# A one-core decoder trunk: table loads on two queues, VectorE's order in the first row and at a pass border, norm vectors as columns, and the last layer norm in pieces with tanh

## The reference, cut to what matters

```
mod = silu(c) @ w_ada + b_ada                 # 1024 -> 6 x 1024: sh1, sc1, g1, sh2, sc2, g2
h = rms_norm(x, norm1_g) * (1 + sc1) + sh1
qa, ka, va, ub, uc, ud = split(h @ w_in)      # q, k, v | conformer | short conv | pool
ya = diff_attention(qa, ka, va, ...)          # 4 heads, two score maps each, causal
yb = silu(layer_norm(dwconv31(val * sigmoid(gate)) + dw_b, ln_g, ln_b))   # 256 channels
yc = bg * dwconv3(cg * xc)
yd = multiscale_pool(ud) @ pool_w * pool_scale
x = x + g1 * (concat(ya, yb, yc, yd) @ w_out)
h = rms_norm(x, norm2_g) * (1 + sc2) + sh2
x = x + g2 * (square(relu(h @ w_ff1)) @ w_ff2)
```

## Time and profile before

| | before |
|---|---|
| three runs, us | 2376.82 (median), 2379.27, 2375.77 |
| profiled execution, us | 2375.63 |
| its span, us | 2373.8 |
| granted TensorE clock, mean of the span | 0.987 |
| PE busy | 2285.4 us, 96% |
| DVE busy | 1749.2 us, 74% |
| ACT busy | 975.2 us, 41% |
| POOL busy | 354.6 us, 15% |
| chain that ended last, by engine | PE 83%, DVE 8%, DMA 3%, ACT 2% |

### The profile page before, as it was taken

One profiled execution on the slowest core, in us unless ns is written; L12 is line 12 of the kernel. 1 busy time (PEld: TensorE's weight loads), 2 busy tenths in 40 slices (PEclk: granted clock), 3 DMA queues, 4 the chain that ended last, 5 costly groups with the idle time before them and its releaser, 6 DMA issues.

```text
span 2373.8 us, 31336 instructions
## 1 busy us (share of the span) xinstructions
PE 2285.4 (96%) x11618; PEld 1926.3 (81%) x11618; DVE 1749.2 (74%) x2660; ACT 975.2 (41%) x1598; POOL 354.6 (15%) x281
## 2 busy tenths in 40 slices
PE   5999999987999999999999999999999999999999
PEld 3987897766889888888888888888888888888887
DVE  5558796978989876877676767677687676767676
ACT  4532555458888854432322222233432322223231
POOL 0343043823355630000000000000000000000000
PEclk8999999988999999999999999999999999999999
DMA  7441434120000052111111111135101111111112
GB/s 261 156 155 46 151 116 151 49 98 27 15 14 23 10 163 77 54 54 36 62 44 55 51 53 53 53 123 195 63 28 44 62 44 53 53 53 53 53 53 88
DMA packets 108280, 177.68 MB, mean 75 GB/s; under 512 B 5512, under 2 KB 77468, under 8 KB 107164
## 3 DMA queue, kind: packets, MB, share of 16 engines
q1 hardware_dynamic: 108188, 176.45, 22.5%
HBM read 152.84 MB, written 23.59 MB: 74 GB/s over the span
## 4 chain that ended last, share of the span: by engine, by line
PE 83%; DVE 8%; DMA 3%; ACT 2%; issue 2%; POOL 1%; SPq 1%; ACTq 0%; DVEq 0%
PE ps L2486 10%; PE ps L2484 10%; PE ps L2485 10%; PE ps L2522 7%; PE ps L2521 7%; PE ps L2523 7%; PE ps L2187 6%; PE ps L2188 6%; PE ps L2189 6%; PE ps L2374 2%; PE ps L2431 2%; PE ps L2429 2%; PE ps L2430 2%; PE ps L2359 2%; DVE sb_scores L1816 2%
## 5 line engine op out<-in xcount | busy, mean ns | idle before, releaser
L1974 DVE TENSOR_TENSOR sb_x_new<-sb_x_new,ps 128x512 f32<-128x512 f32 x512 | 347.2, 684 | 107.6 <-PE ps L2486 102.0
L2484 PE MATMUL ps<-sb_w_hi,sb_u_hi 128*128 128x512 f32 x1024 | 398.3, 389 | 0.0
L2485 PE MATMUL ps<-sb_w_lo,sb_u_hi 128*128 128x512 f32 x1024 | 398.3, 389 | 0.0
L2486 PE MATMUL ps<-sb_w_hi,sb_u_lo 128*128 128x512 f32 x1024 | 398.3, 389 | 0.0
L2486 PEld LDWEIGHTS ps<-sb_w_hi,sb_u_lo 128*128 128x128 f32 x1024 | 192.3, 188 | 39.9
L2484 PEld LDWEIGHTS ps<-sb_w_hi,sb_u_hi 128*128 128x128 f32 x1024 | 192.3, 188 | 39.9
L2485 PEld LDWEIGHTS ps<-sb_w_lo,sb_u_hi 128*128 128x128 f32 x1024 | 192.3, 188 | 39.8
L2189 PE MATMUL ps<-sb_h_hi,sb_w_lo 128*128 128x512 f32 x512 | 199.4, 389 | 0.0
L1418 ACT ACTIVATE ps<-ps 128x512 f32<-128x512 f32 x28 | 16.3, 582 | 410.8 <-PE ps L2523 410.8
L2187 PE MATMUL ps<-sb_h_hi,sb_w_hi 128*128 128x512 f32 x448 | 178.0, 397 | 0.7 <-DVE sb_w_lo L1935 0.7
L2188 PE MATMUL ps<-sb_h_lo,sb_w_hi 128*128 128x512 f32 x448 | 174.4, 389 | 0.0
(11 more groups left out here) (286 smaller groups left out, 4955.4 us busy)
## 6 DMA issues: line engine op xcount, KB each, us to landing
sb_w_full<-in_w_ff SPq DMA_DIRECT2D x34, 1024.0 KB, 5.1
sb_w_full<-in_w_ff SPq DMA_DIRECT2D x56, 512.0 KB, 3.8
sb_w_raw<-in_w_in SPq DMA_DIRECT2D x16, 1024.0 KB, 5.7
sb_ada<-in_w_ada SPq DMA_DIRECT2D x32, 512.0 KB, 5.3
sb_ada_first<-in_w_ada SPq DMA_DIRECT2D x8, 1024.0 KB, 14.3
sb_x_in<-in_x SPq DMA_DIRECT2D x16, 512.0 KB, 4.9
sb_mix_in<-mix_scratch SPq DMA_DIRECT2D x16, 512.0 KB, 5.1
sb_x_new<-in_x SPq DMA_DIRECT2D x16, 512.0 KB, 4.8
```

The costliest lines, as they stand in the source:

```text
L1974: V.tensor_tensor(out=y, in0=y, in1=psum[:, 4 + p % 4, :], op=ALU.add).then_inc(ff2_read, 1)
L2484: M(dst, uh, wh[:, j, col], start=j == order[0], stop=False, skip_group_check=fast)
L2485: M(dst, uh, wl[:, j, col], start=False, stop=False, skip_group_check=fast)
L2486: ins = M(dst, ul, wh[:, j, col], start=False, stop=j == order[1], skip_group_check=fast)
```

## The change

Six things are moved or replaced; all numbers of the result stay as the reference has them.

- The five tables for the conformer and short convolution, biases and weights, are loaded from ACT's queue, ahead of its first table load, and no longer from SP's. The lambda load goes behind the first `w_ada` slab.
- In the chain of the first row, `w_lo` of the first slab comes behind DVE's gain and no longer ahead of the column extraction; PE transposes the first x tile behind slab 5 and no longer behind slab 7.
- At the end of pass one, the statistics, the row tail and the scaling of the x tiles (`load_squares`, `h_tail`, `scale_rows`) move ahead of three taps and of the short convolution of the next block.
- The shift and gain vectors of the second norm come as eight one-column products of PE, and DVE reads the eight columns directly.
- `load_qk(2)` goes ahead of the store of layer norm (1, 0), and `load_qk(3)` directly behind the load of v.
- Layer norm (1, 1): the reciprocal runs as four pieces of 128 columns, in steps 9 to 12; its two products in steps 13 and 14; ACT's part, one channel half each in steps 16 and 17. In pass two, `Tanh` of half the argument takes the place of `Sigmoid`, and POOL makes 0.5 t + 0.5 of it with a `tensor_scalar` ahead of each product. Its POOL part stands at u = 19 in place of 10, its store behind `load_qk(8)` in place of `load_qk(6)`.

```diff
-                                (R_DWB, R_LNG, conf_dw_b), (R_LNG, R_LNB, conf_ln_g),
-                                (R_LNB, R_PSC, conf_ln_b), (R_PSC, R_END1, pool_scale)):
+                                (R_PSC, R_END1, pool_scale)):
                 sp.dma_start(table1[r0:r1, :], rows(src)).then_inc(tab_ld, 16)
-            for r0, r1, src in ((R_DWW, R_SW, conf_dw_w), (R_SW, R_END2, short_conv_w)):
-                sp.dma_start(table2[r0:r1, :], src.rearrange("o j (a p) -> (o j a) p", p=P)).then_inc(tab_ld, 16)
...
-            sp.dma_start(lam_in[:, :, :], lam_params[0, :, :].partition_broadcast(P)).then_inc(lam_ld, 16)
             for k in range(DC):
                 sp.dma_start(ada_first[k][:, :], w_ada_v[:, k, 0:2 * D]).then_inc(ada0_ld[k], 16)
+                if k == 0:
+                    sp.dma_start(lam_in[:, :, :], lam_params[0, :, :].partition_broadcast(P)).then_inc(lam_ld, 16)
...
+            load_qk(2)
             store_ln(1, 0)
...
             sp.dma_start(v_sb[:, :, :], qkv_v[:, :, 2 * GW:3 * GW]).then_inc(v_ld, 16)
+            load_qk(3)
             sp.dma_start(gate_d[:, :], gate_row[:, 0, :]).then_inc(gate_st, 16)
-            for i in range(2, NT):
+            for i in range(4, NT):
                 load_qk(i)
-                if i == 6:
+                if i == 8:
                     store_ln(1, 1)
...
                     y = acc[:, cc, b * BLK:(b + 1) * BLK]
+                    if h:
+                        half = ln_sig[h][cc][:, :]
+                        link(pool.tensor_scalar(half, half, 0.5, 0.5, ALU.mult, ALU.add))
                     pool.tensor_tensor(out=y, in0=y, in1=ln_sig[h][cc][:, :], op=ALU.mult).then_inc(lnout_ready, 1)
...
-                if u == LN_STEP + 4:
+                if u == LN_STEP + 13:
                     ln_out(1, 1)
...
+            for r0, r1, src in ((R_DWW, R_SW, conf_dw_w), (R_SW, R_END2, short_conv_w)):
+                act.dma_start(table2[r0:r1, :], src.rearrange("o j (a p) -> (o j a) p", p=P)).then_inc(tab_ld, 16)
+            for r0, r1, src in ((R_DWB, R_LNG, conf_dw_b), (R_LNG, R_LNB, conf_ln_g), (R_LNB, R_PSC, conf_ln_b)):
+                act.dma_start(table1[r0:r1, :], src.rearrange("o (a p) -> (o a) p", p=P)).then_inc(tab_ld, 16)
             act.wait_ge(const_ready, 1)
...
-                    A(ln_sig[h][cc][:, :], acc[:, cc, blk], ACT.Sigmoid).then_inc(lnsig_ready, 1)
+                    if h:
+                        A(ln_sig[h][cc][:, :], acc[:, cc, blk], ACT.Tanh, scale=0.5).then_inc(lnsig_ready, 1)
+                    else:
+                        A(ln_sig[h][cc][:, :], acc[:, cc, blk], ACT.Sigmoid).then_inc(lnsig_ready, 1)
...
-                if u == LN_STEP + 4:
-                    ln_silu(1, 1)
+                if u in (LN_STEP + 10, LN_STEP + 11):
+                    ln_silu(1, 1, (u - LN_STEP - 10,))
...
+            def ln_inverse(part):
+                dve.wait_ge(*ln_read(1, 1, 1))
+                rs = ln_rs[1][:, part * P:(part + 1) * P]
+                return mark(V.reciprocal(rs, rs))
+
+            def ln_scale_part(cc, done):
+                y = acc[:, cc, BLK:2 * BLK]
+                dve.wait_ge(dve_chain, done)
+                ins = V.tensor_tensor(out=y, in0=y, in1=ln_rs[1][:, :], op=ALU.mult)
+                if cc == GC - 1:
+                    ins.then_inc(lnz_ready, 1)
...
-                columns(psum[:, 6:8, :], DC, h_tmp[:, :, :].rearrange("p k t -> p (k t)"))
                 r = R_B + (3 + h) * DC
-                vector = V.scalar_tensor_tensor(out=(gain2 if h else shift2)[:, :], in0=diag_sum[:, 0:DC], scalar=float(GW),
+                vector = V.scalar_tensor_tensor(out=(gain2 if h else shift2)[:, :], in0=psum[:, 6, 0:DC], scalar=float(GW),
...
+                    if h == 0 and (cc, b) == (GC - 1, 0):
+                        load_squares(HT + 2)
+                        h_tail(HT, h_tmp)
+                        scale_rows(HT + 2)
                     if h or b == 0:
                         pump(taps, 3)
...
-                    if h == 0 and (cc, b) == (GC - 1, 0):
-                        h_tail(HT, h_tmp)
-                        load_squares(HT + 2)
                     if h == 0 and (cc, b) == (0, 1):
                         h_tail(HT + 1, h_tmp)
-                        scale_rows(HT + 2)
...
-                if u == LN_STEP + 3:
-                    ln_scale(1, 1)
+                if 0 <= u - LN_STEP - 3 < 4:
+                    inverted = ln_inverse(u - LN_STEP - 3)
+                if 0 <= u - LN_STEP - 7 < GC:
+                    ln_scale_part(u - LN_STEP - 7, inverted)
...
+                if k == 5:
+                    transposes(0, x_in[0])
             ins.then_inc(mod1_mm, 1)
-            pe.wait_ge(tab_col, 2)
-            transposes(0, x_in[0])
...
-                for n in range(2):
-                    ins = M(psum[:, 6 + n, :], ones_mean[:, :], mod_sums(h)[1 - s][:, n * BLK:(n + 1) * BLK], start=True, stop=True)
+                if s:
+                    for n in range(2):
+                        ins = M(psum[:, 6 + n, :], ones_mean[:, :], mod_sums(h)[0][:, n * BLK:(n + 1) * BLK], start=True, stop=True)
+                else:
+                    for k in range(DC):
+                        ins = M(psum[:, 6, k:k + 1], mod_sums(h)[1][:, k * P:(k + 1) * P], ones_mean[:, 0:1], start=True, stop=True)
```

More of the change, by code:

```diff
@@ L1554, in _ @@
             add_slice(7)
-            w_in_tail(0)
             dve.wait_ge(mod1_mm, 1)
@@ L1563, in _ @@
                                    op0=ALU.add, op1=ALU.mult).then_inc(mod1_ready, 1)
+            w_in_tail(0)
             V.memset(conf[:, :, 0:TAPS - 1], 0.0)
```

6 lines of the change are left out of this document (3 added, 3 removed).

## The result

The changed kernel took 2357.9 us (median of four runs, 2356.4 to 2361.4); the kernel before it 2378.05 in the same measurement. The ratio is 0.9913 with a 95% interval of 0.9896 to 0.9931. A second measurement of the same code gave 0.9894 (0.9876 to 0.9913). The forecast was 2360.0 with a range of 2352 to 2368. The profiled execution's span fell from 2373.8 to 2354.6 us, by 19.2, and TensorE's mean granted clock rose from 0.987 to 0.993.

What follows compares the result with a forecast made beforehand. TensorE was taken as busy almost throughout, losing time to a few waits in the first 900 us. Terms -7.0 - 1.5 - 2.5 - 2.3 - 3.0 = -16.3 from 2375.63 gave 2359.3, stated as 2360.0 us, range 2352 to 2368.

Steps and rivals of the forecast that it cites:

- Start: Kernel start: earlier DMA stream and reordered first-row chain let PE begin projections at about 40.1 us, -7.0 us.
- Border: Border of the two passes: PE's 5.29 us wait goes, but what follows is late next, -1.5 us.
- Norm vectors: Pass two: two DVE instructions of 1.22 us each go ahead of the gated products PE waits for, -2.5 us.
- rival b: Start gives less: stream doesn't move, or more first projections run at PE's lower clock; 2362 to 2365 us, chance 0.14.
- Attention's start: Head of attention: earlier q/k tile ends ACT's wait, only DVE's idle 2.65 us on the path, -2.3 us.
- Last layer norm: Attention around steps 10 to 12: 9.6 us lost there go, pieces, Tanh and POOL's work cost some back, -3.0 us.
- Rival (c): DVE and POOL's shared port lock: layer norm gives nothing or costs up to 3.5 us; 2363 to 2366.5, chance 0.16.
- (d): Attention gains more, ACT's 6.8 us and most of the 9.6 coming through; 2349 to 2355 us, chance 0.08.
- (e): Start slower: tables issued by ACT queue behind the slabs on the shared DMA engines; up to 2379 us, chance 0.05.

Runs made afterwards that it cites:

- u_tables: Changed kernel with all ten tables back on SP's queue and the lambda load ahead of the first slab again: 2359.95 us, ratio 0.9917.
- u_chain: Changed kernel with `w_lo` ahead of the column extraction and PE's first-row transposes behind slab 7 again: 2363.27 us, ratio 0.9929.
- the repeat: The changed kernel executed and traced once more, no edit: 2356.95 us, ratio 0.9894.
- u_border: Changed kernel with statistics, tail and scaling of the x tiles back behind the taps and the short convolution: 2360.51 us, ratio 0.9924.
- u_norm: Changed kernel with the norm vectors as two products of 512 columns and DVE's column extraction again: 2361.72 us, ratio 0.9930.
- after: The first profiled execution of the changed kernel, no further edit: span 2354.6 us; the kernel's median time 2357.9 us.
- u_qk: Changed kernel with the third and fourth q/k tile loaded behind the layer-norm store, value load and gate store again: 2365.26 us, ratio 0.9926.
- s_sig: Changed kernel with Sigmoid for Tanh in both layer norms of pass two, without POOL's four extra instructions; pieces stay: 2364.63 us, ratio 0.9920.
- before: The profiled execution of the kernel without the change: span 2373.8 us; the kernel took 2378.05 us in the same measurement.

## Why the prediction was right

The sum (-16.3) and the time came out near the measured -19.2 and 2357.9, by the mechanisms named; two of the five terms were clearly too small, a third can't be told apart from what executions differ by, and the errors partly cancel, so that the sum comes as near as this is in part luck. (2359.3 and the 1.2 to the median make 2360.5; the forecast says 2360.0.)

- **Start, -7.0: right.** 7.11 at the first projection, by the rows forecast; u_tables and u_chain share it as 2.3 and 5.4. The 0.9 more in the first rows was not in the sum, and the repeat doesn't have it (0.05).
- **Border, -1.5: right.** 1.0, and 1.65 by u_border. The x tile that I named as late next is the wait; the value weights were not. The mechanism is seen; the -1.5 itself was set between 0 and -5.3 and not worked out.
- **Norm vectors, -2.5: mis-sized.** The term counted DVE's 2.44 us and took PE's clock as given. It measured 4.1, and 4.95 in u_norm. The rest is the lower clock behind the longer wait, which the prediction takes up only as a loss at the start (rival b). In two of ten traces with the changed order the clock fell here all the same.
- **Attention's start, -2.3: not told apart.** 1.0 in after, 1.9 in the repeat; u_qk gives 1.63 for the loads against after and 2.54 against the repeat. DVE's idle 2.65 us did go. POOL's two extra instructions hold PE's first score for 0.9 (I had said 0.4), but s_sig, without them, has none of that left at place 6. What after lacks against the repeat it loses where its four sums of the layer norm run at the lower clock (3.38 against 2.13 us).
- **Last layer norm, -3.0: mis-sized.** 5.2. I counted 9.6 lost and 6.6 given back. By PE's starts 8.7 were won (13.9 at place 6, 22.6 at the product that starts at 549.65 in before) and 3.6 given back by place 7: the term that failed is what the pieces, Tanh and POOL's part cost in the dense steps. POOL's new instruction costs 0.62, not 1.25; how the rest divides no run shows. Before, the granted clock around this hole was 0.68, 0.50 and 0.50 from 540 to 555, after it was 1.00 from 515 to 565; the sum had no term for that.

Rival (c), the lock: its mechanism is seen. The Trainium skill ("SBUF — State Buffer", Who interferes with whom) has DVE and GpSimd block each other on a shared port pair. The trace agrees, and with the full price: in after the ratio instruction takes over 0.3 us ten times between 505 and 745, and each time it ends 0.01 to 0.02 us behind a POOL instruction. It is held until POOL is done, so it pays what is left of POOL's instruction and not always a whole 1.3, and the other 40 of 50 take at most 0.27, so the layer norm still gained. Rivals (d) and (e) didn't come.

Open: what makes the granted clock fall behind one wait of 2.0 to 2.7 us and not behind the same wait in another execution. The runs show that it does both, not why.
